# Values held still in two FP32R halves: the prompt attention of a hybrid decoder step, from its second tile on

## The reference, cut to what matters

```python
def _sparse_attend(q, k_sel, v_sel, valid):
    logits = einsum('btkgd,btnkd->btkgn', qg, k_sel) * (HEAD_DIM ** -0.5)
    logits = where(valid[:, :, None, None, :], logits, NEG_INF)
    p = softmax(logits, axis=-1)
    o = einsum('btkgn,btnkd->btkgd', p, v_sel)
    return o.reshape(b, t, ATT_DIM)

def _layer(...):
    ...
    branch_b = attend(q, qi, wi, k, v, ki) * silu(z_b)
    merged = sigmoid(g_a) * (branch_a @ w_pa) + sigmoid(g_b) * (branch_b @ w_pb)
    y = x + gate * (merged @ w_out)
```

## Time and profile before

| | |
|---|---|
| median of three runs | 3245.71 us (3241.59 to 3247.2) |
| profiled execution | 3244.32 us, its span 3242.5 us |
| TensorE busy | 3164.9 us, 98% |
| VectorE busy | 1879.8 us, 58% |
| ScalarE busy | 1100.5 us, 34% |
| GpSimd busy | 839.2 us, 26% |
| granted TensorE clock, mean | 0.996 |
| value products of tiles 1 to 3 | 2016 instructions, 263.9 us |
| transposes of probabilities | 1088 instructions, 166.7 us |
| DMA | 592.52 MB, mean 183 GB/s |

### The profile page before, as it was taken

How to read it: one execution, slowest core, us unless ns; L and a number is a source line. 1 busy time by engine, 2 the same in 40 slices (tenths; PEclk the granted TensorE clock), 3 DMA queues, 4 the chain that set the end, 5 groups by cost and what they waited for, 6 DMA issues and landing times.

```text
span 3242.5 us, 48134 instructions
## 1 busy us (share of the span) xinstructions
PE 3164.9 (98%) x18999; PEld 2745.4 (85%) x18999; DVE 1879.8 (58%) x3640; ACT 1100.5 (34%) x1956; POOL 839.2 (26%) x765
## 2 busy tenths in 40 slices
PE   7999999999899999999999999999999999999999
PEld 6999999956888888888887888889888788889987
DVE  5443695044535993035257999056437899947652
ACT  3444332345324221154244221154226322135431
POOL 2345675444510332012200331100310133010011
PEclk9999999999999999999999999999999999999999
DMA  8765678674874555622744556610563455650017
GB/s 299 252 213 197 223 274 288 242 250 153 295 236 156 198 193 207 233 97 77 255 160 154 195 192 210 229 35 11 201 212 120 158 195 198 218 187 11 9 37 238
DMA packets 262353, 592.52 MB, mean 183 GB/s; under 512 B 17485, under 2 KB 174343, under 8 KB 212466
## 3 DMA queue, kind: packets, MB, share of 16 engines
q1 hardware_dynamic: 251620, 551.57, 50.0%
q0 software_dynamic: 10368, 37.75, 3.5%
q10 hardware_dynamic: 142, 0.13, 0.0%
HBM read 448.93 MB, written 140.47 MB: 182 GB/s over the span
## 4 chain that ended last, share of the span: by engine, by line
PE 91%; DVE 3%; ACT 2%; DMA 1%; POOL 1%; issue 1%; ACTq 0%; SPq 0%; DVEq 0%; POOLq 0%
PE ps L1162 84%; PE ps L1167 7%; DMA WR<-in_w_proj_b 1%; DVE RS L1828 1%; POOL BBL L2425 0%; DMA GB<-gb_scratch 0%; DVE XN L1749 0%; ACT SC L921 0%; DVE LP L2090 0%; POOL WLH L2264 0%; DVE OB L2101 0%; DMA WR<-in_w_in 0%; DMA ST<-in_state_conv 0%; DVE sKPT L2014 0%; ACT JUNK L733 0%
## 5 line engine op out<-in xcount | busy, mean ns | idle before, releaser
L1162 PE MATMUL ps<-HTH,WLH 128*128 128x512 f32 x3504 | 1128.0, 390 | 0.0
L1162 PEld LDWEIGHTS ps<-HTH,WLH 128*128 128x128 f32 x3504 | 657.9, 188 | 139.2 <-issue 5.0
L1162 PE MATMUL ps<-HTL,WLH 128*128 128x512 f32 x1752 | 682.0, 389 | 0.0
L1961 DVE TENSOR_SCALAR_CACHE_REDUCE JUNK<-SC,SMALL 128x384 bf16<-128x384 f32 (+13 forms) x392 | 580.0, 1479 | 15.6 <-POOL sSC L2350 1.7
L1162 PE MATMUL ps<-H,WLH 128*128 128x288 f32 x3504 | 483.8, 299 | 4.8 <-DVE H L1788 2.0
L1162 PEld LDWEIGHTS ps<-H,WLH 128*128 128x128 f32 x3504 | 474.2, 191 | 6.7 <-issue 2.4
L1162 PEld LDWEIGHTS ps<-HTL,WLH 128*128 128x128 f32 x1752 | 329.1, 188 | 65.3
L2090 DVE CUSTOM_DVE_ANT_0 LP<-ps,SC,RQ 128x512 f32<-128x512 f32 (+3 forms) x320 | 201.7, 667 | 294.1 <-ACT SC L921 277.6
L885 ACT ACTIVATE T<-ps 128x512 f32<-128x512 f32 x192 | 115.0, 599 | 701.5 <-PE ps L1162 698.1
L2264 POOL TENSOR_TENSOR WLH<-WR,WLH 128x1024 fp32r<-128x1024 f32 x97 | 236.2, 2435 | 319.4 <-ACT WLH L708 319.3
L1162 PE MATMUL ps<-V,T 128*128 128x128 f32 x2016 | 263.9, 276 | 0.8 <-ACT T L1030 0.8
(11 more groups left out here) (344 smaller groups left out, 4544.2 us busy)
## 6 DMA issues: line engine op xcount, KB each, us to landing
WLH<-w_scratch SPq DMA_DIRECT2D x291, 1024.0 KB, 4.8
w_scratch<-WLH SPq DMA_DIRECT2D x97, 1024.0 KB, 5.7
WR<-in_w_in SPq DMA_DIRECT2D x73, 512.0 KB, 4.3
MW<-in_w_mod SPq DMA_DIRECT2D x6, 2048.0 KB, 16.2
q_scratch<-QO SPq DMA_DIRECT2D x32, 256.0 KB, 5.6
ma_scratch<-T SPq DMA_DIRECT2D x32, 256.0 KB, 5.6
gb_scratch<-GB SPq DMA_DIRECT2D x32, 256.0 KB, 5.6
QU<-q_scratch SPq DMA_DIRECT2D x64, 128.0 KB
```

The costliest lines, as they stand in the source:

```text
L1162: return pe.matmul(out, lhsT, rhs, start=start, stop=stop, **more)
L1961: ins_ = dve.tensor_scalar(JUNK[0:n, 0:row.shape[1]], row, MID[0:n, c:c + 1], 0.0, ALU.is_ge, ALU.add, accum_out=CNT[0:n, c:c + 1])
```

## The change

From tile 1 on, the value products are made like the other products, in FP32R halves, and with the operands' parts exchanged: values stand still, turned probabilities of both heads (256 columns) move. The result then has features by queries and is not turned back. The division by the row sums comes with a matrix of ones times a diagonal matrix of the reciprocals, which spreads a query's reciprocal over all features. What that takes:

- values: GpSimd splits each tile's new values into high halves (in place of V) and low halves, which SP stores to HBM (vl_scratch) and, ahead of each attention, loads into two of the three weight buffers. The two weights that would have been there are loaded after the last value product, ahead of gates and x.
- probabilities: ScalarE copies all groups from PSUM, rounding to FP32R (PTH). The low half (PTL) is PSUM minus PTH on VectorE; for groups c = 3 and 7 of units 0 to 13 ScalarE makes a second, exact copy and GpSimd subtracts.
- order: the transposes run two groups ahead of the values instead of one; VectorE's subtraction of group 0 stands ahead of the last mask piece of the next unit; those of groups 1 and 2 behind it, the others behind finish.
- sums: VectorE also splits the reciprocals, GpSimd multiplies the unit matrix by them (diagonals), TensorE adds two 256-column products (lengths) in turn_out's place; finish becomes two operations, and scale goes.

```diff
-                for hh in range(2):
-                    ins_ = mm(ps[acc][:, hh * HD:(hh + 1) * HD], PT[t][p_slot(t, u, c)][:, (2 * kk + hh) * P:(2 * kk + hh + 1) * P],
-                              V[:, k, (pr // 2) * HD:(pr // 2 + 1) * HD], k == 0 and hh == 0, k == n - 1, skip_group_check=True)
+                if t:
+                    if u == 0 and k in (0, 8):
+                        pe.wait_ge(*vl_in[k // 8].at(t))
+                        pe.wait_ge(*v_low.at(t, 1))
+                    cols = slice(2 * kk * P, 2 * (kk + 1) * P)
+                    out = ps[acc][:, 0:256]
+                    mm(out, VR[:, k, head], PTH[slot][:, cols], k == 0, False, skip_group_check=True)
+                    mm(out, VR[:, k, head], PTL[slot][:, cols], False, False, skip_group_check=True)
+                    ins_ = mm(out, VL[t][k // 8][:, k % 8, head], PTH[slot][:, cols], False, k == n - 1, skip_group_check=True)
+                    continue
...
+            turn_p(t, u, 1)
             for c in range(groups):
-                if c + 1 < groups:
-                    turn_p(t, u, c + 1)
+                if c + 2 < groups:
+                    turn_p(t, u, c + 2)
+                if last and c == groups - 1:
+                    lengths(t, u)
                 group_values(t, u, c)
...
+        def lengths(t, u):
+            acc = acc_bank(t, u)
+            pe.wait_ge(*diag.at(t, u))
+            for part_ in range(2):
+                ins_ = mm(ps[acc][:, 256:512], ones[:, :].bitcast(F32R), DG[:, 2 * part_:2 * part_ + 2, :].rearrange("p h q -> p (h q)"),
+                          part_ == 0, part_ == 1, skip_group_check=True)
+            ins_.then_inc(*turned.mark(t, u))
...
+    low_on_pool = lambda t, u, c: c % 4 == 3 and u < len(UNITS) - 2
...
+            act.activation((PTH if t else PT[t])[slot][:, 0:m], src, ACT.Copy).then_inc(*p_copy_a.mark(t, u, c))
+            if t and low_on_pool(t, u, c):
+                act.activation(PTW[slot][:, 0:m], src, ACT.Copy).then_inc(*p_raw.mark(t, u, c))
...
+        def probabilities_low(t, u, c):
+            if low_on_pool(t, u, c):
+                return
...
+            dve.wait_ge(*p_copy_a.at(t, u, c))
+            dve.tensor_tensor(PTL[slot][:, 0:m], ps[bank("tr", t, u, c)][:, 0:m], PTH[slot][:, 0:m].bitcast(F32), ALU.subtract
+                              ).then_inc(*p_low_dve.mark(t, u, c))
...
             for u in range(len(UNITS)):
                 if u + 1 < len(UNITS):
                     mask_logits(t, u + 1)
+                else:
+                    probabilities_low(t, u, 0)
+                groups = unit_groups(t, u)
+                for c in (1, 2):
+                    probabilities_low(t, u, c)
                 unit_sum(t, u)
                 if u:
                     finish(t, u - 1)
-                n = BLOCKS * t + UNITS[u][0] + 1
-                for c in range((n + 1) // 2):
-                    if on_act(t, u, c):
-                        continue
...
+                for c in range(3, groups):
+                    probabilities_low(t, u, c)
                 for b, r in late_runs(t, u):
                     choose(t, scores(t)[:, b, 0:width(BLOCKS * t + b)], P, b, b, r)
-                scale(t, u)
...
+                sp.wait_ge(*pv.at(t, len(UNITS) - 1))
+                for h in range(2):
+                    if BLOCKS * (t + 1) > 8 * h:
+                        load_w(first + len(PROJ_A) + len(PROJ_B) + 1 + h)
```

More of the change, by code:

```diff
@@ L384, in program @@
     xr_in = [signal(f"xr_in{i}", 16) for i in range(2)]
-    table_in, table_row, piece, kx_dup = signal("table_in", 16), signal("table_row"), signal("piece"), signal("kx_dup")
+    table_in, kx_dup = signal("table_in", 16), signal("kx_dup")
     kx_in = [signal(f"kx_in{i}", 16) for i in range(2)]
-    pg_in = [signal(f"pg_in{i}", 16) for i in range(19)]
+    pg_in = {i: signal(f"pg_in{i}", 16) for i in sorted(set(PAGE_SLOT))}
     q_out = [signal(f"q_out{i}", 16) for i in range(2)]
@@ L618, in _ @@
                 j = first + len(PROJ_A) + i
-                if j + 3 not in AFTER_PAGES:
+                h = i - (len(PROJ_B) - 2)
+                if t and h >= 0 and BLOCKS * (t + 1) > 8 * h:
+                    load_vl(t, h)
+                elif j + 3 not in AFTER_PAGES:
                     load_w(j + 3)
+                if t and i in (3, 4):
+                    store_vl(t, i - 3)
                 if j + 2 not in AFTER_PAGES:
@@ L2088, in mask_logits @@
                 for x, (c, n) in enumerate(runs):
+                    if t and u and hh and x == len(runs) - 1:
+                        probabilities_low(t, u - 1, 0)
                     dve.wait_ge(*qk.at(t, u, hh, c))
@@ L2377, in convolve, with value_halves, first_value_halves, diagonals @@
                 pool.tensor_tensor(x[0], x[0], x[4], ALU.mult).then_inc(*conv.mark(t, f, p))
+        def value_halves(t, f):
+            pool.wait_ge(*a_done.at(t, PROJ_A.index(("v", f)), "P"))
+            four = lambda ap: ap.rearrange("p (b d) -> p b d", b=BLOCKS)
+            place = VR[:, BLOCKS * t:BLOCKS * (t + 1), f * HD:(f + 1) * HD]
+            link(pool.tensor_copy(place, four(VO[f][:, :])))
+            pool.tensor_tensor(four(VLO[f][:, :]), four(VO[f][:, :]), place.bitcast(F32), ALU.subtract).then_inc(*v_low.mark(t, f))
+        def first_value_halves(f):
+            if f == 0:
+                pool.wait_ge(*pv.at(0, len(UNITS) - 1))
+                pool.wait_ge(*v_out.at(0, 1))
+                pool.wait_ge(*merged.at(0, KC - 1, "P"))
+            two = lambda ap: ap.rearrange("p (b d) -> p b d", b=2)
+            whole, high = V[:, 2 * f:2 * f + 2, :], two(VH0[f][:, :])
+            link(pool.tensor_copy(high, whole))
+            link(pool.tensor_tensor(two(VLO0[f][:, :]), whole, high.bitcast(F32), ALU.subtract))
+            pool.tensor_copy(VR[:, 2 * f:2 * f + 2, :], high.bitcast(F32)).then_inc(*v_low.mark(0, f))
+        def diagonals(t, u):
+            pool.wait_ge(*scaled.at(t, u))
+            if u:
+                pool.wait_ge(*turned.at(t, u - 1))
+            pool.tensor_tensor(DG[:, :, :], ident[:, :].unsqueeze(1).to_broadcast([P, 4, P]),
+                               R4[u % 2].unsqueeze(2).to_broadcast([P, 4, P]), ALU.mult).then_inc(*diag.mark(t, u))
+        def probabilities_low(t, u, c):
+            if not low_on_pool(t, u, c):
+                return
+            m = 256 * min(2, BLOCKS * t + UNITS[u][0] + 1 - 2 * c)
+            slot = p_slot(t, u, c)
+            pool.wait_ge(*p_raw.at(t, u, c))
+            pool.tensor_tensor(PTL[slot][:, 0:m], PTW[slot][:, 0:m], PTH[slot][:, 0:m].bitcast(F32), ALU.subtract
+                               ).then_inc(*p_low_pool.mark(t, u, c))
         def branch_low(f):
+            if t and f == 2:
+                pool.wait_ge(*vl_out.at(t, 1))
+                pool.wait_ge(*v_out.at(t, 1))
             if t == 0 and f == KC - 2:
@@ L2478, in _ @@
                         query_low(t, u + 2)
+                    for c in range(unit_groups(t, u)):
+                        probabilities_low(t, u, c)
+                        if c == min(3, unit_groups(t, u) - 1):
+                            diagonals(t, u)
                     if u == len(UNITS) - 2 and t + 1 < TILES:
@@ L2493, in _ @@
                     h_low(t + 1, f)
+                if t == 0 and f in (2, 4):
+                    first_value_halves(f // 2 - 1)
                 j += 1
```

111 lines of the change are left out of this document (80 added, 31 removed).

## The result

Before: 3247.0 us (median of 5 runs). After: 3267.6 us (median of 5, 3260.0 to 3272.0). Ratio 1.0071, 95% interval 1.0060 to 1.0082: the change makes the kernel 0.7% slower. Forecast: 3256, within 3212 to 3284; the direction and the range hold, the size is 12 us short.

What follows compares the result with a forecast made beforehand. TensorE, with 91% of the span, was taken to bound the kernel; its 47 us saving would turn into waits and a little more: 3244.3 + 10 (attention stages) + 2 (weights) = 3256 us, range 3212 to 3284.

Steps and rivals of the forecast that it cites:

- TensorE's saving: Value products of tiles 1 to 3: 0.351 us a block in place of 0.445, 504 blocks, 47 us saved.
- Busy time: Sign to look for in the changed profile: TensorE busy time down by some 45 us.
- the distances between units: Sign: units 1 to 7 of tile 3 at 15 to 16.5 us; wrong if they stay below 14.5.
- The feed outside units 0 to 7 of tile 3: Waits for copies and subtractions against the saving: tile 1 +1.6, tile 2 -2.3, tile 3's units 8 to 15 about -1.5 us.
- The schedule: Unit-by-unit layout of the engines' queues in the three attention stages: +10 us in sum; chance 0.40 for 3252 to 3270.
- The waits ahead of value products: Sign: TensorE idle for subtractions 0.2 to 1.3 us a time, some 40 to 60 us over the three stages.
- the schedule's waits: Waits over the three attention stages: 47 + 10 = 57 us.
- Units 0 to 7 of tile 3: VectorE also runs the late selection there: +1.5 us a unit, eight units, +12; bounds +6 and +16.
- Weights after attention: Second, third and fourth w_proj_b weights loaded late after each attention: +2 us in all, bounds 0 and +9.
- The full feed: Rival: feed holds, saving comes through: 3213 us, or 3227 with half the waits; chance 0.25; without any wait 3197.
- rival two: GpSimd and VectorE collide on one port in tile 3's first eight units (+10), weights late (+7): 3266 to 3273; chance 0.15.

Runs made afterwards that it cites:

- experiment 4: Changed kernel without the low half of the probabilities (no subtraction, no second ScalarE copy; same number of products, high half used twice): 3201.8 us.
- experiment 1: Changed kernel, leaving out all but the last operation of each late selection piece in units 0 to 7 of tile 3: 3247.1 us.
- experiments 1 and 9: 9: low product last, late selection spread at four operations over each of tile 3's first ten units: 3229.9 us; also GpSimd subtracting in fewer units: 3223.5 us.
- experiment 6: Changed kernel with the low product last (3248.6 us) plus 17.5 us of added products ahead of the wait in tile 3: 3240.2 us.
- experiment 3: Changed kernel plus 17.5 us of value-neutral products before tile 3's mask wait: median 3264.7 us; its unit pair, same code without added products: 17.80 and 16.42 us.
- experiment 7: Low product last, tile 3's late selection put between the subtractions, group 5's subtraction moved to GpSimd: 3243.5 us; with that move undone, 9 us faster.

## Why the prediction was right or wrong

**TensorE's saving: right.** Value products came every 0.117 us, and 46 us are saved when nothing is late (experiment 4). But TensorE's busy time fell by 11 us, not 45: at 1.2 GHz the same products count as longer, and the first product of a block lasts 0.32 us on average where the other two last 0.28. It fell by 21 us where tile 3's clock stayed at 1.00 (experiment 1) and by 41 without the subtractions (experiment 4). Busy time was the wrong witness, and the chain's share would be no better, as the chain covers 78% of the span here and 99% before; the distances between units were the right one.

**The feed outside units 0 to 7 of tile 3: right by units, 1 to 2 us off by tile.** The schedule gave +1.6 for tile 1, -2.3 for tile 2 and -1.5 for tile 3's last eight units (its listed steps times four add up to +1.8, -2.9 and -0.8). Measured are +3.8, -0.3 and 0.0, each with 0.5 us for the end of attention, below. Unit by unit the schedule is right within 0.4 us: 5 blocks took 6.11 us (forecast 6.1), 9 blocks 10.42 (10.15), 16 blocks 16.9 (16.87). The waits ahead of value products, 17.5 us, are fewer than the 40 to 60 forecast, but idle time on TensorE is a part of the lateness only: its weight loads wait 36.6 us. By stages (experiment 4) the feed costs 73 us in all, 39 of them outside these eight units; the schedule's waits came to 57.

**Units 0 to 7 of tile 3: the step that was mis-sized.** "+1.5 a unit, eight units: +12", bounded by 16. Measured is +23.7, the whole of the stage's loss (150.7 us against 127.0); five of the seven distances lie above the 15 to 16.5 us that were forecast. Its mechanism, VectorE with masks, subtractions and selection in one queue, is right (experiments 1 and 9). Two parts are missing. VectorE's round is longer than laid out: with added products and the clock at 1.00 these units still take 16.4, not 15.4, where the selection's last operation takes 1.1 us in place of 0.69 in five of eight units, those in which it starts behind GpSimd's low half of the queries, and where VectorE waits 15 us in the eight units, 1.9 each, for ScalarE's copies (the schedule has some 0.6 a unit, an estimate from its times). How the two share the difference was not tested. And I let TensorE come back from a 2.5 us wait at the clock at which it went in. After five of the eight waits (1.86 to 2.47 us) its products fell to the 1.2 GHz level 1.2 to 2.0 us after it went on, not after those of 2.32, 1.73 and 1.13, nor, without the scan, after 0.74. The profiles with added products price that at 8 us of the stage, the ten executions of experiment 6 at 8.4, and the pair of units in experiment 3 at 1.4 us a unit.

**Weights after attention: wrong in place, near in size.** The eight w_proj_b products end 44.6 to 45.4 us after the first one's start in the three tiles, before 44.6, and TensorE waits for none of their weights: no weight is late. What came is ahead of the first product. At the end of tile 1's attention, of the kernel after:

```profile
1525.47 0.76 PE L1215 MATMUL ps<-BBH,WLH 128*128 128x512 f32 x1 [2.00 <-POOL BBL L2565]
```

It is 2.00 us in every tile. The 0.35 of the earlier trace rows is not its counterpart, since before there was the last unit's turn back, with a wait of 0.70, in the same place: from the end of the last value product to this product it was 1.5 us. So 0.5 us a tile is lost here, 1.5 in all (the forecast was +2, for the weights), inside the stages above. In both kernels the product waits for GpSimd's first low half of the attention output, which starts when the last value product ends. The low halves by tile, of the kernel after:

```profile
L2246 DVE TENSOR_TENSOR BBL<-BB,BBH x12: 692/1365/1781, 1523.5 to 3174.4; 128x512 fp32r<-128x512 f32 x12
L2565 POOL TENSOR_TENSOR BBL<-BB,BBH x12: 1721/1738/1777, 1523.6 to 3175.6; 128x512 fp32r<-128x512 f32 x12
```

The same place in the timeline of the kernel before, GpSimd and then VectorE:

```profile
1521.75 6.36 POOL L2425 TENSOR_TENSOR BBL<-BB,BBH 128x512 fp32r<-128x512 f32 x4 [6.85 <-PE ps L1162]
...
1522.23 1.33 DVE L2146 TENSOR_TENSOR BBL<-BB,BBH 128x512 fp32r<-128x512 f32 x1
```

Before, GpSimd started first and its first low half took 1.27 us; VectorE, behind its division by the row sums, started second and took 1.33. Now VectorE has no division to do, starts 0.05 us ahead of GpSimd (1523.51 and 1523.56) and takes 0.69, and GpSimd takes 1.72 or more. I had priced no such collision at this place.

**Rivals.** The full feed did not come (experiment 4 is what it would have been: 3201.8, my bound without any wait was 3197). The collisions of rival two were 0.4 us in five of the eight units here, not 1.3 in each, because the selection ran when GpSimd's subtraction was over. Put beside it (experiment 7), they have the size that I had worked out and more. The Trainium skill (SBUF — State Buffer, Who interferes with whom) says that a VectorE instruction with two SBUF inputs contends with a GpSimd one that reads SBUF, and that tensor_scalar can contend too, in its two-port modes, a condition that the prediction left out. The traces agree for the first operation (0.48 to 1.0 us, one SBUF tile) and the running sum (1.28 to 2.19); the subtractions, one input from PSUM, kept 0.68.

**Left open.** Why the clock falls after one wait of 2.3 us and not after another, or after a wait of 2.47 us in one execution and not in another (experiment 3). And why the added products gained 8 us in two profiles but 3 in the median of nine executions: the profiled execution of the changed kernel was one of its two longest, and those with added products were the shortest and the second shortest of their runs, at a mean clock of 0.995 against 0.992 to 0.994 in the others, so a part of the 8 may be the choice of execution.

## What to carry to other kernels

Moving work off the engine that bounds a kernel pays only where the engines that take it have room in that very stretch: lay out their queue for the fullest unit, and look for the burst that stands between two things the bounding engine needs. A wait of TensorE of some 2 us can cost another 1.4 to 1.6 at the lower clock behind it (17.80 against 16.42 for the same wait; 18.2 against 16.6 with added products), so cut the longest wait first: thin the burst, or order products so that those with the late operand go last. Handing an operation to GpSimd can slow VectorE by more than it takes away.

## What the hardware showed that was not expected

- Work added to TensorE, 17.5 us of it, made the kernel 8.4 us faster (3248.6 to 3240.2): in the profiled execution 512-column products stayed at 0.23 us in place of 0.43.
- VectorE's running sum of 512 columns took 2.19 us beside a GpSimd subtraction, 1.28 without one; that subtraction, which had started behind another VectorE operation, took 1.72 in place of 1.28.
- Where VectorE and GpSimd collided, it was the one that started second that took longer: the selection's last operation took 1.09 us when it started 0.2 to 0.3 us behind GpSimd's low half of the queries, 0.69 when it started 0.09 ahead, and then GpSimd took 1.18 in place of 0.73.
